# A softmax-attention front in the order queries, keys, values, with the cosine products in PSUM

## The chip, the cores and the metric

The kernel runs on one core of one Trainium2 chip. The metric is the device time of one execution in microseconds (us). Engines are named as in the profile: PE is TensorE (PEld its weight loads), DVE is VectorE, ACT is ScalarE, POOL is GpSimd, SP is SyncE.

## The reference, cut to what matters

The program is a whole stack of blocks over 512 tokens of width 1024. The change is in one mixer, which computes a multi-scale pooling and a grouped-query attention side by side from one input:

```python
z = h @ w_in                       # pooled inputs u (512), q (512), k (128), v (128)
pooled = multiscale_pool(u)        # 4 windows, one for each 128 channels
a = (pooled @ w_pool + b_pool) * pool_scale
q = apply_rope(rms_norm_2(q) * q_gain, cos, sin)    # 8 heads of 64
k = apply_rope(rms_norm_2(k) * k_gain, cos, sin)    # 2 heads of 64
p = softmax(q @ k.T * Dh ** -0.5)
y = concatenate([a, p @ v]) @ w_out
```

`apply_rope` turns even and odd channels into each other: the cosine product of the normalised input plus the sine product of its rotated copy.

## The kernel before

Activations lie with channels on the partitions and the 512 tokens along the row. Every projection is done in three passes (high times high, low times high, high times low part), all as 128x512 matmuls, except the values: those come out token-major directly, as 4 x 24 matmuls of 128 columns (kind "KV", L537).

Weights come in chunks of 256 output channels through two slots. For each chunk SP loads `raw`, ACT writes its high part `wh` (`hi_part`, L475, which waits until the chunk two before has been multiplied), and POOL writes its low part `wl` (L2164, 4.6 us for a full chunk). TensorE writes a chunk's result into one of two pairs of PSUM banks, `pairs`; four further banks are `aux`. Semaphores order everything; each engine runs its own list in the order in which the code issues it, so the functions `front_pe`, `front_act`, `front_dve` and `att_pe`, `att_act`, `att_dve` are those orders written out by hand. `linear_pe` is the general projection, with a hook `mid` between the two halves of a chunk.

Three chains (x = 0, 1, 2) normalise and rotate: before, the keys are x = 0, query tiles 0 and 1 are x = 1, query tiles 2 and 3 are x = 2. A chain is: Square on ACT, mean square on TensorE (`rope_ms_pe`, L1487), Ln and Exp on ACT (`rope_rs_act`), on DVE the normalised input qn (L1522) and the cosine product (L1526), the rotation on TensorE (`rope_rot_pe`, L1495), and on DVE the sine product (L1532) and the sum (L1537; for the keys four half-height copies, L1541). An fp32 matmul of 512 columns is two instructions in the trace, so one 1024-column mean square or rotation is "x4".

The pooling runs beside it: window sums on DVE (`pool_u_dve`, L1435 to L1444), a product on TensorE (`pool_pe`, L1450), bias and scale on DVE (L1455), high part on ACT (L1465) and low part on DVE (L1460).

The attention loop has 16 steps n, each over one pair of heads and 128 tokens: `scores` (L1576), row maximum (L1701), exponential with sum (L1639), reciprocal and multiply (L1711, L1714), eight transposes (`turn`, L1589), copy (L1648), and every second step the product with the values (`values`, L1601). Scores of step n+2 are issued before turn n. In the kernel before, chain x = 2 lies inside this loop: its mean square after the first two scores, its rotation after turn 1, its DVE parts in steps 0 and 1.

Of the kernel before, what the change touches and what calls it, by code (L numbers as in the profile page):

```python
# [20 lines left out]
P = 128  # L21
T = 512
# [28 lines left out]
for _name, _w in (("ones", P), ("ident", P), ("ntri", P), ("nones", P), ("neg_strict", P), ("keep_strict", P),  # L51
# [18 lines left out]
          ("pool_u", "F", 2), ("att_kv", "KV", 1), ("att_q", "F", 2), ("att_out", "F", 4),  # L70
# [21 lines left out]
def build(nc, xT, w2048, w1024, w1408, ada, c_d, par_d, cst_d, gla_d, rope_d, pool_d, outT):  # L92
    with ExitStack() as ctx:
# [1310 lines left out]
        AK = arena[:, 21, :]  # L1404
# [41 lines left out]
        def pool_pe(p, g):  # L1446
            p.wait_ge(u_pooled, g + 1)
            if g >= 2:
                p.wait_ge(u_out, g - 1)
            p.matmul(aux[:, g % 2, :], WPOOL[:, g * P:(g + 1) * P], UP[:, g, PAD:PAD + T], start=True, stop=True  # L1450
                     ).then_inc(u_mm, 1)

        def pool_out_dve(v, g):
            v.wait_ge(u_mm, g + 1)
            v.tensor_scalar(UP[:, g, PAD:PAD + T], aux[:, g % 2, :], pc("b_pool", g), pc("pool_scale", g),  # L1455
                            ALU.add, ALU.mult).then_inc(u_out, 1)
# [10 lines left out]

        r_sq, r_ms, r_ln, r_rs, r_qn = sem("r_sq"), sem("r_ms"), sem("r_ln"), sem("r_rs"), sem("r_qn")
# [5 lines left out]

        ROPE_SRC = [AK.rearrange("p (a t) -> p a t", a=1), AQ[:, 0:2, :], AQ[:, 2:4, :]]
        ROPE_W = [1, 2, 2]
        ROPE_MS = [aux[:, 2:3, :], aux[:, 0:2, :], aux[:, 0:2, :]]
        ROPE_ROT = [aux[:, 3:4, :], aux[:, 2:4, :], aux[:, 2:4, :]]

        def rope_ms_pe(p, x):  # L1480
            p.wait_ge(r_sq, x + 1)
            if x == 1:
                p.wait_ge(u_out, 4)
            elif x == 2:
                p.wait_ge(r_ln, 2)
            for i in range(ROPE_W[x]):
                mm = p.matmul(ROPE_MS[x][:, i, :], cm("bd64"), A_SQ[:, i, :], start=True, stop=True)  # L1487
            mm.then_inc(r_ms, 1)

        def rope_rot_pe(p, x):  # L1490
            p.wait_ge(r_qn, x + 1)
            if x:
                p.wait_ge(r_t2, x)
            for i in range(ROPE_W[x]):
                mm = p.matmul(ROPE_ROT[x][:, i, :], cm("rot"), A_QN[:, i, :], start=True, stop=True)  # L1495
            mm.then_inc(r_rot, 1)

        def rope_sq_act(a, x):
            a.wait_ge(drained, (C_KV + 1, C_Q + 1, C_Q + 2)[x])
            if x:  # L1500
                a.wait_ge(r_out, x)
            a.activation(A_SQ[:, 0:ROPE_W[x], :], ROPE_SRC[x], ACT.Square).then_inc(r_sq, 1)

        def rope_rs_act(a, x):
            a.wait_ge(r_ms, x + 1)
            rs = A_RS[:, 0:ROPE_W[x], :]
            a.activation(rs, ROPE_MS[x], ACT.Ln, scale=1.0 / 64, bias=pc("eps")).then_inc(r_ln, 1)
            a.wait_ge(r_ln, x + 1)
            a.activation(rs, rs, ACT.Exp, scale=-0.5).then_inc(r_rs, 1)

        def rope_by(x):
            return 1.0 if x else SB_D ** -0.5
# [4 lines left out]
        def rope_qn_dve(v, x):  # L1517
            v.wait_ge(r_rs, x + 1)
            if x:
                v.wait_ge(r_rot, x)  # L1520
            qn = A_QN[:, 0:ROPE_W[x], :]
            v.scalar_tensor_tensor(qn, ROPE_SRC[x], pc("q_gain" if x else "k_gain"), A_RS[:, 0:ROPE_W[x], :],  # L1522
                                   ALU.mult, ALU.mult).then_inc(r_qn, 1)
            v.wait_ge(r_qn, x + 1)
            v.wait_ge(rope_in, 16)
            v.scalar_tensor_tensor(A_T1[:, 0:ROPE_W[x], :], qn, rope_by(x), rope_table(0, x), ALU.mult, ALU.mult  # L1526
                                   ).then_inc(r_t1, 1)

        def rope_out_dve(v, x):
            v.wait_ge(r_rot, x + 1)  # L1530
            t1, t2 = A_T1[:, 0:ROPE_W[x], :], A_T2[:, 0:ROPE_W[x], :]
            v.scalar_tensor_tensor(t2, ROPE_ROT[x], rope_by(x), rope_table(1, x), ALU.mult, ALU.mult  # L1532
                                   ).then_inc(r_t2, 1)
            v.wait_ge(r_t1, x + 1)
            v.wait_ge(r_t2, x + 1)
            if x:
                v.tensor_tensor(ROPE_SRC[x], t1, t2, ALU.add).then_inc(r_out, 1)  # L1537
            else:
                for kv in range(2):
                    for r in (0, 64):  # L1540
                        ins = v.tensor_tensor(AKD[r:r + 64, kv, :], t1[kv * 64:kv * 64 + 64, 0, :],  # L1541
                                              t2[kv * 64:kv * 64 + 64, 0, :], ALU.add)
                ins.then_inc(r_out, 1)
# [5 lines left out]

        def front_pe(p):  # L1550
# [5 lines left out]
            rope_rot_pe(p, 0)  # L1556
            pool_pe(p, 2)
            pool_pe(p, 3)
            linear_pe(p, "att_q", lo=1, mid=lambda: rope_ms_pe(p, 1))
            rope_rot_pe(p, 1)  # L1560

        def att_pe(p):
            def scores(n):
                pr, tb = n // TB, n % TB
                if n == 0:
                    p.wait_ge(drained, C_Q + 1)
                    p.wait_ge(r_out, 2)
                elif n == 1:
                    p.wait_ge(drained, C_Q + 2)
                else:  # L1570
                    p.wait_ge(e_p, 2 * (n - 1))
                    if n == 2 * TB:
                        p.wait_ge(r_out, 3)
                for j in range(2):
                    r = 64 * j
                    mm = p.matmul(pairs[:, 2 * e_slot(n) + j, :], AQ[r:r + 64, pr, tb * P:(tb + 1) * P],  # L1576
                                  AKD[r:r + 64, pr // 2, :], start=True, stop=True)
                mm.then_inc(scored, 1)

            def turn(n):  # L1580
                p.wait_ge(e_pn, n + 1)
                if n:
                    p.wait_ge(e_tc, n)
                else:
                    p.wait_ge(r_ln, 3)
                for j in range(2):
# [21 lines left out]
            rope_ms_pe(p, 2)  # L1608
            for n in range(AN):
                if n + 2 < AN:  # L1610
                    scores(n + 2)
                turn(n)
                if n == 1:
                    rope_rot_pe(p, 2)
                if n % 2 == 0 and n:
                    values(n // 2 - 1)
            values(AN // 2 - 1)

        def front_act(a):
            hi_only(a, "att_kv")  # L1620
            pool_out_act(a, 0)
            pool_out_act(a, 1)
            hi_part(a, C_Q + 1, (C_Q + 1) % 2)
            rope_sq_act(a, 0)
            rope_rs_act(a, 0)
            hi_part(a, C_Q + 2, (C_Q + 2) % 2)
            rope_sq_act(a, 1)
            pool_out_act(a, 2)
            pool_out_act(a, 3)
            rope_rs_act(a, 1)  # L1630

        def att_act(a):
# [34 lines left out]
        def front_dve(v):  # L1667
            pool_u_dve(v, 0)
            pool_u_dve(v, 1)
            v.wait_ge(mm_done, C_KV + 1)  # L1670
            slot = C_KV % 2
            v.tensor_copy(AK, pairs[:, 2 * slot, :])
            v.tensor_copy(AV, pairs[:, 2 * slot + 1, :].rearrange("p (b n) -> p b n", n=P)).then_inc(drained, 1)
            pool_out_dve(v, 0)
            pool_out_dve(v, 1)
            pool_lo_dve(v, 0)
            pool_lo_dve(v, 1)
            rope_qn_dve(v, 0)
            v.wait_ge(mm_done, C_Q + 1)
            slot = C_Q % 2  # L1680
            v.tensor_scalar(AQ[:, 0:2, :], pairs[:, 2 * slot:2 * slot + 2, :], 1.0, None, ALU.mult).then_inc(drained, 1)
            pool_out_dve(v, 2)
            pool_out_dve(v, 3)
            rope_out_dve(v, 0)
            pool_lo_dve(v, 2)
            pool_lo_dve(v, 3)
            rope_qn_dve(v, 1)
            v.wait_ge(mm_done, C_Q + 2)
            slot = (C_Q + 1) % 2
            v.tensor_scalar(AQ[:, 2:4, :], pairs[:, 2 * slot:2 * slot + 2, :], 1.0, None, ALU.mult).then_inc(drained, 1)  # L1690
            rope_out_dve(v, 1)

        def att_dve(v):
# [13 lines left out]
            for n in range(AN):  # L1707
# [737 lines left out]
```

## Time and profile before

| | |
|---|---|
| median of 3 runs | 1947.4 us (1946.45 to 1948.06) |
| profiled execution | 1948.57 us, span 1946.8 us |
| PE busy | 1906.2 us (98%) |
| DVE busy | 913.0 us (47%) |
| ACT busy | 744.1 us (38%) |
| POOL busy | 770.5 us (40%) |
| granted TensorE clock, mean | 0.995 |

The span is what the trace covers; the execution's own time is 1.8 us longer. Matmuls are pipelined and their ends are modelled, so that PE's share says that it has always something to do, not that it is at its peak. The chain of waits says more: it is the path that ended last, with the engine on it at each moment.

### The profile page before, as it was taken

To read this page: it belongs to the slowest core of one execution; us is meant where nothing else is said; L and a number is where in the kernel's file an instruction comes from. 1 tells how busy PE (TensorE), PEld (TensorE's weight loads), DVE (VectorE), ACT (ScalarE), POOL (GpSimd) and SP (SyncE) were. 2 spreads that over 40 slices of the span, in tenths; PEclk is the share of its full clock that TensorE was granted. 3 is DMA by queue.
4 is the path that set the end of the run, shared out by engine and by line. 5 is a ranking of instruction groups with operands and counts; after the bars stand their busy time and mean duration, and the time that the engine had idled before them with its cause. 6 is when DMAs were issued, how large, how long until landed. Compare 5 with 4: busy or idle time off the path is not lost.

```text
span 1946.8 us, 24500 instructions
## 1 busy us (share of the span) xinstructions
PE 1906.2 (98%) x9346; PEld 1552.1 (80%) x9346; DVE 913.0 (47%) x1227; ACT 744.1 (38%) x931; POOL 770.5 (40%) x227
## 2 busy tenths in 40 slices
PE   7999999999999999979999999999999999999999
PEld 5877778878888888745888888888998778888887
DVE  5344533676614654866676415637855371111111
ACT  5444434443322335336432222234358452222221
POOL 3232314434444435200434343444486434344433
PEclk9999999999999999989999999999999999999999
DMA  5121212445435534200445345422221222223222
GB/s 200 65 75 55 78 53 66 172 151 198 149 117 195 194 119 149 85 1 9 154 184 209 110 148 212 166 96 95 96 95 63 89 105 87 88 96 109 93 78 99
DMA packets 46365, 223.90 MB, mean 115 GB/s; under 512 B 4928, under 2 KB 9280, under 8 KB 31696
## 3 DMA queue, kind: packets, MB, share of 16 engines
q1 hardware_dynamic: 33184, 174.85, 26.1%
q10 hardware_dynamic: 13104, 47.98, 6.5%
q8 instruction: 53, 0.87, 0.2%
q14 instruction: 24, 0.20, 0.0%
HBM read 220.68 MB, written 2.13 MB: 114 GB/s over the span
## 4 chain that ended last, share of the span: by engine, by line
PE 83%; DVE 5%; issue 5%; POOL 4%; ACT 2%; DMA 1%; SPq 0%; ACTq 0%; DVEq 0%; POOLq 0%
PE pairs L518 40%; PE pairs L546 18%; PE pairs L1088 4%; PE pairs L570 4%; PE pairs L537 3%; PE pairs L862 3%; PE pairs L855 2%; POOL arena L1923 2%; POOL wl L2164 2%; PE pairs L496 1%; PE aux L1601 1%; DMA raw<-in_w 1%; PE aux L920 1%; DVE aux L454 1%; DVE xl L461 1%
## 5 line engine op out<-in xcount | busy, mean ns | idle before, releaser
L2164 POOL TENSOR_TENSOR wl<-raw,wh 128x2048 fp32r<-128x2048 f32 (+2 forms) x169 | 695.5, 4115 | 1121.8 <-ACT wh L475 1121.8
L518 PE MATMUL pairs<-xh,wh 128*128 128x512 f32 x1176 | 460.3, 391 | 3.8 <-DVE aux L748 1.5
L518 PE MATMUL pairs<-xh,wl 128*128 128x512 f32 x1176 | 457.7, 389 | 0.0
L518 PE MATMUL pairs<-xl,wh 128*128 128x512 f32 x1176 | 457.7, 389 | 0.0
L475 ACT ACTIVATE wh<-raw 128x2048 fp32r<-128x2048 f32 x171 | 326.7, 1911 | 318.6 <-PE pairs L546 209.1
L518 PEld LDWEIGHTS pairs<-xh,wh 128*128 128x128 f32 x1176 | 220.9, 188 | 52.0 <-issue 3.4
L518 PEld LDWEIGHTS pairs<-xh,wl 128*128 128x128 f32 x1176 | 220.9, 188 | 47.2 <-issue 1.2
L518 PEld LDWEIGHTS pairs<-xl,wh 128*128 128x128 f32 x1176 | 220.9, 188 | 45.9
L546 PE MATMUL pairs<-zl,wh 128*128 128x512 f32 x518 | 201.6, 389 | 0.0
L546 PE MATMUL pairs<-zh,wl 128*128 128x512 f32 x518 | 201.5, 389 | 0.0
L546 PE MATMUL pairs<-zh,wh 128*128 128x512 f32 x518 | 201.5, 389 | 0.0
L787 DVE SCALAR_TENSOR_TENSOR arena<-arena,cond_row 128x1024 f32<-128x1024 f32 x96 | 188.2, 1992 | 0.0
L748 DVE TENSOR_TENSOR aux<-arena,pairs 128x512 f32<-128x512 f32 x66 | 45.9, 696 | 226.9 <-ACT arena L711 211.8
L711 ACT ACTIVATE arena<-pairs 128x512 f32<-128x512 f32 x42 | 25.1, 598 | 323.0 <-PE pairs L518 304.2
L633 DVE SCALAR_TENSOR_TENSOR h<-pairs,mod,h 128x512 f32 (+1 forms) x48 | 36.0, 751 | 226.0 <-PE pairs L546 179.5
L546 PEld LDWEIGHTS pairs<-zh,wh 128*128 128x128 f32 x518 | 97.2, 188 | 20.4
L546 PEld LDWEIGHTS pairs<-zh,wl 128*128 128x128 f32 x518 | 97.2, 188 | 20.2
L546 PEld LDWEIGHTS pairs<-zl,wh 128*128 128x128 f32 x518 | 97.2, 188 | 20.1
L751 DVE TENSOR_TENSOR zl<-aux,zh 128x512 f32 (+1 forms) x66 | 45.7, 692 | 92.3 <-ACT zh L716 92.3
L229 ACT ACTIVATE arena<-h 128x512 f32<-128x512 f32 (+1 forms) x48 | 30.1, 626 | 90.2 <-DVE h L633 59.8
L632 DVE TENSOR_TENSOR h<-pairs,h 128x512 f32 (+1 forms) x24 | 16.6, 692 | 96.7 <-PE pairs L546 81.1
L254 DVE TENSOR_TENSOR arena<-arena 128x512 f32<-128x512 f32 x48 | 54.3, 1132 | 3.4 <-ACT arena L229 3.4
(322 smaller groups left out, 2944.0 us busy)
## 6 DMA issues: line engine op xcount, KB each, us to landing
raw<-in_w SPq DMA_DIRECT2D x113, 1024.0 KB, 4.9
arena<-in_ada ACTq DMA_DIRECT2D x88, 512.0 KB, 5.4
raw<-in_w SPq DMA_DIRECT2D x48, 704.0 KB, 4.1
raw<-in_w SPq DMA_DIRECT2D x14, 512.0 KB, 3.6
arena<-in_ada SPq DMA_DIRECT2D x8, 512.0 KB, 4.9
arena<-mx_rows SPq DMA_DIRECT2D x16, 256.0 KB, 3.5
h<-in_xT SPq DMA_DIRECT2D x4, 512.0 KB, 9.0
outT<-h SPq DMA_DIRECT2D x8, 256.0 KB, 5.5
```

The costliest lines, as they stand in the source:

```text
L254: v.tensor_tensor(SQ_ACC, SQ_ACC, SQ[slot], ALU.add).then_inc(sq_acc, 1)
L475: a.activation(wh[:, slot, :], raw[:, slot, :], ACT.Copy).then_inc(hi_done, 1)
L518: mm = p.matmul(pairs[:, 2 * slot + m, :], w[:, slot, at:at + P], src[part][:, k, :], start=(k == 0 and w is wh and part == 0), stop=(k == ...
L537: mm = p.matmul(dst, src[part][:, k, tb * P:(tb + 1) * P], w[:, slot, at:at + n], start=(k == 0 and w is wh and part == 0), stop=(k == KT ...
L546: mm = p.matmul(pairs[:, 2 * slot + m, :], w[:, slot, k * P:(k + 1) * P], src[part][:, k, :], start=(k == ks[0] and w is wh and part == 0) ...
L570: mm = p.matmul(pairs[:, 2 * slot + m, :], w[:, slot, at:at + P], src[part][:, k, :], start=(k == ks[0] and w is wh and part == 0), stop=( ...
L748: v.tensor_tensor(HID[:, slot, :], ACTV[:, slot, :], pairs[:, 2 * slot + 1, :], ALU.mult).then_inc(hid_done, 1)
L751: v.tensor_tensor(zl[:, bass.ds(l, 1), :], HID[:, slot:slot + 1, :], zh[:, bass.ds(l, 1), :].bitcast(F), ALU.subtract).then_inc(drained, 1)
L787: v.scalar_tensor_tensor(ada_raw[:, at, :], ada_raw[:, at, :], 1.0, cond_row[:, :], ALU.mult, ALU.mult, accum_out=mod_raw[:, bass.ds(A, 1) ...
L862: mm = p.matmul(out, w[:, slot, at:at + P], x[:, k, :], start=(k == 0 and w is wh and x is xh), stop=(k == KT - 1 and x is xl))
L1088: mm = p.matmul(pairs[:, 2 * slot + m, :], w[:, slot, at:at + P], x[:, k, :], start=(k == 0 and w is wh and x is xh), stop=(k == KT - 1 an ...
L2164: g.tensor_tensor(wl[:, slot, 0:w], raw[:, slot, 0:w], wh[:, slot, 0:w].bitcast(F), ALU.subtract).then_inc(lo_done, 1)
```

## The change

- The chunks come in the order queries, keys and values. The chains are renumbered: query tiles 0 and 1 are x = 0, tiles 2 and 3 are x = 1, the keys x = 2. All three chains are now in the front; the loop keeps only pooling low parts and the second keys' head, on DVE in step 0.
- Queries and keys are no longer copied from `pairs` to SBUF: Square and qn read the PSUM banks, and the cosine products of the query chains are written into PSUM.
- The values are projected as the keys are, channel-major in 24 matmuls of 512 columns; ACT copies them to SBUF, TensorE turns them in four transposes, and ACT copies the result to `AV`. The first scores wait for the first of these copies (they write the same bank), the first turn for the last.
- TensorE's projections are cut in quarters (`q_pe`, `kv_pe` with `k0`, `k1`) with the chains' matmuls between them. Ln of chain 0 also waits for the fourth window's pooling, whose work space it reuses.

```diff
-          ("pool_u", "F", 2), ("att_kv", "KV", 1), ("att_q", "F", 2), ("att_out", "F", 4),
+          ("pool_u", "F", 2), ("att_q", "F", 2), ("att_kv", "KV", 1), ("att_out", "F", 4),
...
+        ROPE_SRC = [Q_BANKS[0], Q_BANKS[1], K_BANK]
...
+        ROPE_T1 = [ROPE_MS[0], Q_BANKS[1], arena[:, 26:27, :]]
...
         def rope_rs_act(a, x):
             a.wait_ge(r_ms, x + 1)
+            if x == 0:
+                a.wait_ge(u_pooled, 4)
...
+        def kv_pe(p, m, k0=0, k1=KT):
+
+            slot = C_KV % 2
+            if m == 0 and k0 == 0:
+                p.wait_ge(lo_done, C_KV + 1)
+                p.wait_ge(r_qn, 1)
+            for k in range(k0, k1):
+                for w, x in ((wh, xh), (wl, xh), (wh, xl)):
+                    at = k * 256 + m * P
+                    mm = p.matmul(V_BANK if m else K_BANK[:, 0, :], w[:, slot, at:at + P], x[:, k, :],
+                                  start=(k == 0 and w is wh and x is xh), stop=(k == KT - 1 and x is xl))
+            if k1 == KT:
+                mm.then_inc(mm_done if m else kv_half, 1)
+
+        def v_turn_pe(p):
+            p.wait_ge(drained, C_KV + 1)
+            p.wait_ge(r_ln, 3)
+            for tb in range(TB):
+                mm = p.transpose(V_TURN[:, tb * P:(tb + 1) * P], A_VT[:, tb * P:(tb + 1) * P], cm("ident"))
+            mm.then_inc(v_turned, 1)
 
         def front_pe(p):
             linear_pe(p, "pool_u", norm="n_final")
-            linear_pe(p, "att_kv")
+            q_pe(p, 0, 0)
+            q_pe(p, 0, 1)
             pool_pe(p, 0)
             pool_pe(p, 1)
-            linear_pe(p, "att_q", hi=1, mid=lambda: rope_ms_pe(p, 0))
+            q_pe(p, 1, 0, 0, 4)
+            rope_ms_pe(p, 0)
+            q_pe(p, 1, 0, 4, 8)
+            q_pe(p, 1, 1, 0, 4)
             rope_rot_pe(p, 0)
+            q_pe(p, 1, 1, 4, 8)
+            kv_pe(p, 0, 0, 4)
+            p.wait_ge(r_out, 1)
             pool_pe(p, 2)
             pool_pe(p, 3)
-            linear_pe(p, "att_q", lo=1, mid=lambda: rope_ms_pe(p, 1))
+            rope_ms_pe(p, 1)
+            kv_pe(p, 0, 4, 8)
+            kv_pe(p, 1, 0, 4)
+            rope_ms_pe(p, 2)
             rope_rot_pe(p, 1)
+            kv_pe(p, 1, 4, 8)
+            rope_rot_pe(p, 2)
+            v_turn_pe(p)
...
                 if n == 0:
-                    p.wait_ge(drained, C_Q + 1)
                     p.wait_ge(r_out, 2)
+                    p.wait_ge(drained, C_KV + 1)
                 elif n == 1:
-                    p.wait_ge(drained, C_Q + 2)
+                    p.wait_ge(r_out, 3)
...
+            a.wait_ge(mm_done, C_KV + 1)
+            a.activation(A_VT, V_BANK, ACT.Copy).then_inc(drained, C_KV + 1 - C_Q)
+            a.wait_ge(v_turned, 1)
+            a.activation(AV, V_TURN.rearrange("p (b n) -> p b n", n=P), ACT.Copy).then_inc(v_copied, 1)
```

ACT's list from the last `hi_part` of the normalisation on, before and after (L475 is `hi_part`, L1465 a pooling high part; old L1502, L1507 and L1509 are Square, Ln and Exp, and so are new L1517, L1524 and L1526):

```order
 L475 ACTIVATE wh<-raw 128x2048
+L1517 ACTIVATE arena<-pairs 128x1024
+L475 ACTIVATE wh<-raw 128x2048
+L1524 ACTIVATE arena<-aux,par 128x1024
+L1526 ACTIVATE arena<-arena 128x1024
 L1465 ACTIVATE zh<-arena 128x512 x2
-L475 ACTIVATE wh<-raw 128x2048
-L1502 ACTIVATE arena<-arena 128x512
-L1507 ACTIVATE arena<-aux,par 128x512
-L1509 ACTIVATE arena<-arena 128x512
```

The Square of the first query chunk and the high part of the keys' chunk now stand ahead of the pooling high parts, and Ln and Exp of chain 0 too.

DVE's list at the start of the attention loop in the kernel before, from the sum of chain 1 on:

```order
L1537 TENSOR_TENSOR arena<-arena 128x1024
L1701 TENSOR_REDUCE small<-pairs 128x2 x2
L1711 RECIPROCAL small<-small 128x2
L1714 TENSOR_SCALAR arena<-arena,small 128x512 x2
L1522 SCALAR_TENSOR_TENSOR arena<-arena,par 128x1024
L1526 SCALAR_TENSOR_TENSOR arena<-arena 128x1024
L1701 TENSOR_REDUCE small<-pairs 128x2
L1711 RECIPROCAL small<-small 128x2
L1714 TENSOR_SCALAR arena<-arena,small 128x512 x2
L1532 SCALAR_TENSOR_TENSOR arena<-aux,arena 128x1024
L1537 TENSOR_TENSOR arena<-arena 128x1024
```

and the same place after the change (L1767, L1777 and L1780 are row maximum, reciprocal and multiply, L1460 the pooling low parts, L1562 the second keys' head):

```order
L1555 TENSOR_TENSOR arena<-pairs,arena 128x1024
L1767 TENSOR_REDUCE small<-pairs 128x2 x2
L1777 RECIPROCAL small<-small 128x2
L1780 TENSOR_SCALAR arena<-arena,small 128x512 x2
L1460 TENSOR_TENSOR zl<-arena,zh 128x512 x2
L1562 TENSOR_TENSOR arena<-arena 64x512 x2
L1767 TENSOR_REDUCE small<-pairs 128x2
L1777 RECIPROCAL small<-small 128x2
L1780 TENSOR_SCALAR arena<-arena,small 128x512 x2
```

The four products and sums of the third query chain, of 1024 columns each, are gone from steps 0 and 1; four operations of 512 columns stand in step 0.

## Rows read from the trace of the kernel before

**Rows 1.** Chain of waits, 765 to 945: start, length (us), engine, tile, line.

```profile
796.58 5.44 PE pairs L518 x24
802.02 10.67 PE pairs L537 x96
812.69 1.77 PE aux L1450 x4
814.45 5.49 PE pairs L518 x24
...
845.94 1.73 PE aux L1495 x4
...
886.04 1.22 DVE small L1701
...
887.37 0.89 DVE arena L1714 x2
...
889.40 1.88 PE aux L1601 x16
891.28 1.08 PE pairs L1576 x4
...
892.39 1.22 DVE small L1701
...
920.75 11.13 PE pairs L570 x48
```

**Rows 2.** PE's timeline: start, length, operation [idle before, who ended it].

```profile
836.82 3.22 PE L1487 MATMUL aux<-arena,cst 128*128 128x512 f32 x4 [2.49 <-ACT arena L1502]
...
850.40 3.15 PE L1576 MATMUL pairs<-arena 64*128 64x512 f32 x8 [2.74 <-DVE arena L1537]
...
857.25 1.06 PE L1589 MATMUL aux<-cst,arena 128*128 128x128 f32 x8 [0.24 <-ACT arena L1507]
...
873.08 1.97 PE L1589 MATMUL aux<-cst,arena 128*128 128x128 f32 x8 [3.71 <-DVE arena L1714]
874.98 3.61 PE L1601 MATMUL aux<-arena 128*64 128x256 f32 x16
```

**Rows 3.** DVE's timeline, 785 to 880, the same columns.

```profile
799.00 4.96 DVE L1444 TENSOR_TENSOR arena<-arena 128x512 f32<-128x512 f32 x1
...
808.81 2.92 DVE L1435 TENSOR_TENSOR arena<-arena 128x527 f32<-128x527 f32 x4
...
830.41 5.21 DVE L1541 TENSOR_TENSOR arena<-arena 64x512 f32<-64x512 f32 x4
837.32 1.29 DVE L1460 TENSOR_TENSOR zl<-arena,zh 128x512 fp32r<-128x512 f32 x2 [1.70 <-ACT zh L1465]
...
843.64 1.23 DVE L1526 SCALAR_TENSOR_TENSOR arena<-arena 128x1024 f32<-128x1024 f32 x1
...
847.70 1.23 DVE L1532 SCALAR_TENSOR_TENSOR arena<-aux,arena 128x1024 f32<-128x1024 f32 x1 [0.49 <-PE aux L1495]
```

**Rows 4.** POOL's timeline, 785 to 880: two passes for low parts.

```profile
798.67 4.74 POOL L2164 TENSOR_TENSOR wl<-raw,wh 128x2048 fp32r<-128x2048 f32 x1 [5.53 <-ACT wh L475]
...
828.37 4.59 POOL L2164 TENSOR_TENSOR wl<-raw,wh 128x2048 fp32r<-128x2048 f32 x1 [5.41 <-ACT wh L475]
```

**Rows 5.** ACT's timeline, 785 to 880.

```profile
796.67 1.92 ACT L475 ACTIVATE wh<-raw 128x2048 fp32r<-128x2048 f32 x1 [3.10 <-PE pairs L496]
...
840.08 1.11 ACT L1507 ACTIVATE arena<-aux,par 128x1024 f32<-128x1024 f32 x1 [2.27 <-PE aux L1487]
841.23 1.06 ACT L1509 ACTIVATE arena<-arena 128x1024 f32<-128x1024 f32 x1
...
853.14 0.69 ACT L1639 ACTIVATE arena<-pairs,small 128x512 f32<-128x512 f32 x1 [1.74 <-DVE small L1701]
```

**Rows 6.** Windows: stretch, length, each engine's busy time, granted clock, DMA share, GB/s.

```profile
873.00:875.00 2.00, 1.92 (x10) 1.60 (x10) 1.97 (x5) 0.51 (x2) 0.00 (x0) 0.50 0.04 8
884.00:900.00 16.00, 15.55 (x104) 8.53 (x102) 14.39 (x26) 12.45 (x28) 0.00 (x0) 1.00 0.01 2
```

More of the change, by code:

```diff
@@ L1449, in pool_pe @@
                 p.wait_ge(u_out, g - 1)
[L1450 removed]
+            p.matmul(aux[:, 2 + g % 2, :], WPOOL[:, g * P:(g + 1) * P], UP[:, g, PAD:PAD + T], start=True, stop=True
                      ).then_inc(u_mm, 1)
@@ L1473, in build @@
         AN = ATT_H * TB // 2
[L1475 to L1478, printed above, removed]
+        kv_half = sem("kv_half")
+        Q_BANKS = [pairs[:, 2 * ((C_Q + x) % 2):2 * ((C_Q + x) % 2) + 2, :] for x in range(2)]
+        K_BANK, V_BANK = pairs[:, 2 * (C_KV % 2):2 * (C_KV % 2) + 1, :], pairs[:, 2 * (C_KV % 2) + 1, :]
+        ROPE_SRC = [Q_BANKS[0], Q_BANKS[1], K_BANK]
+        ROPE_W = [2, 2, 1]
+        ROPE_MS = [aux[:, 0:2, :], aux[:, 0:2, :], aux[:, 0:1, :]]
+        ROPE_ROT = [aux[:, 2:4, :], aux[:, 2:4, :], aux[:, 1:2, :]]
+        V_TURN = aux[:, 0, :]
+        ROPE_QN = [A_QN, A_QN, arena[:, 15:16, :]]
+        ROPE_RS = [A_RS, A_RS, arena[:, 16:17, :]]
+        ROPE_SQ = [A_SQ, A_SQ, arena[:, 28:29, :]]
+        ROPE_T1 = [ROPE_MS[0], Q_BANKS[1], arena[:, 26:27, :]]
+        ROPE_T2 = [A_RS, A_RS, arena[:, 27:28, :]]
         def rope_ms_pe(p, x):
@@ L1533, in rope_out_dve, with rope_q_dve @@
                                    ).then_inc(r_t2, 1)
+        def rope_q_dve(v, x):
             v.wait_ge(r_t1, x + 1)
             v.wait_ge(r_t2, x + 1)
[L1536 to L1543, printed above, removed]
+            v.tensor_tensor(AQ[:, 2 * x:2 * x + 2, :], ROPE_T1[x], ROPE_T2[x], ALU.add).then_inc(r_out, 1)
@@ L1546, in e_slot, with rope_k_dve, q_pe @@
+        def rope_k_dve(v, kv):
+            v.wait_ge(r_t1, 3)
+            v.wait_ge(r_t2, 3)
+            half = slice(kv * 64, kv * 64 + 64)
+            for r in (0, 64):
+                ins = v.tensor_tensor(AKD[r:r + 64, kv, :], ROPE_T1[2][half, 0, :], ROPE_T2[2][half, 0, :], ALU.add)
+            ins.then_inc(r_out, 1)
         def e_slot(n):
             return (n + C_Q) % 2
+        def q_pe(p, l, m, k0=0, k1=KT):
+            c = C_Q + l
+            slot = c % 2
+            if m == 0 and k0 == 0:
+                p.wait_ge(lo_done, c + 1)
+                p.wait_ge(drained, c - 1)
+            for k in range(k0, k1):
+                for w, x in ((wh, xh), (wl, xh), (wh, xl)):
+                    at = k * 256 + m * P
+                    mm = p.matmul(pairs[:, 2 * slot + m, :], w[:, slot, at:at + P], x[:, k, :],
+                                  start=(k == 0 and w is wh and x is xh), stop=(k == KT - 1 and x is xl))
+            if m == 1 and k1 == KT:
+                mm.then_inc(mm_done, 1)
```

111 lines of the change are left out of this document (57 added, 54 removed).

## The prediction

> **What bounds the kernel now.** Read the page first: TensorE (PE) is busy nearly all of the span, so a microsecond can only be won where it waits or where its own work shrinks. The change touches one stretch, from the end of the last projection of the pooled inputs (796.58) to the first matmul of att_out (920.75) [rows 1]. Read there the chain of waits. Up to 829 it is TensorE end to end. The keys-and-values chunk costs it 5.44 us for the keys and 10.67 us for the values, which use 96 matmuls of 128 columns [rows 1]. After that the gaps begin; PE's timeline names them. At 836.82 it had waited 2.49 us for ACT's Square of queries 0 and 1, at 850.40 it had waited 2.74 us for DVE's last addition, and at 873.08 3.71 us for the probabilities [rows 2]. The last is in the softmax loop: the third query chain (qn, cosine, rotation, sine, sum of query tiles 2 and 3) sits inside it. Once it is gone, two steps of the loop take 892.39 - 886.04 = 6.35 us, a circle of values, scores, row maximum, multiply and turn, without a longer wait [rows 1]. From turn 0 (857.25) to turn 2 (873.08) they take 15.83 [rows 2].
>
> What to see besides: after such gaps the granted clock is 0.50 of full, the 1.2 GHz level, as in 873 to 875, and it is 1.00 in 884 to 900 [rows 6]. Four matmul instructions that take 1.73 us at full clock [rows 1] then take up to 3.22 [rows 2].
>
> **The front, walked.** I lay durations of rows end to end in the new order of each engine, with about 0.04 us from one engine to the next as the chain shows. The same walk over the old order puts the first scores at 850.42 and the end at 920.85; the trace has 850.40 and 920.75, so the method is good to a few tenths.
>
> PE: from 796.58 two query halves of 5.49 [rows 1] end at 807.5; the pooling products (1.77) [rows 1] and two quarters plus the mean squares plus one quarter (2.74, 1.73, 2.74, 2.74; a quarter is half of 5.49) bring it to 819.2. It then wants the first rotation's input.
>
> ACT: Square of query chunk 0 reads PSUM, 1.08 by L1507's 1.11 and L1509's 1.06 [rows 5], so 807.5 to 808.65; then the high part of the keys' chunk, 1.92 [rows 5], to 810.5.
>
> GpSimd: the low part starts there and takes 4.6 [rows 4], to 815.1. Before, only the pass at 798.67 met the window sums, and no other came before they were done. Now a second one does: DVE is in the fourth window's sums, four L1435 adds from 808.81 [rows 3]. An add with both inputs in SBUF that begins during a GpSimd pass does not end until the pass has: L1444 at 799.00 took 4.96 us and ended at 803.96, the pass at 803.41; the first L1541 at 830.41 had to wait too (four of them took 5.21) for the pass that ended at 832.96 [rows 3, 4]. So the fourth add ends at 815.7 and the last two operations (0.73 each) at 817.2, where the old order had 813.2. The changed Ln of chain 0 waits for all four windows.
> The Trainium skill has this as a rule (SBUF — State Buffer, section SBUF: two separate sides): a DVE op with two SBUF inputs and a GpSimd op take turns on one port pair, each for its whole length. It speaks against this change, and the trace agrees with it by the 4.96 us. Taken to the letter the third add, already running, would also push GpSimd to 811.0 and the sum 0.5 later.
>
> Then Ln and Exp (1.11, 1.06) reach 819.4, qn 1.23, rotation from 820.7 to 822.45. TensorE has waited 1.5 us. From there its own work is 20.6 us: five quarters are 13.7, the pooling products 1.7, mean squares and rotation of queries 2 x 1.73, of keys 2 x 0.86. I checked what it waits for: queries 0 and 1 done 825.6 against 827.9 when needed; second qn 834.9 against 837.7; keys' qn 839.9 against 842.2. It ends at 843.07. DVE's sine and two key copies (0.7 each, by the two L1460 in 1.29 [rows 3]) give the first scores at 845.25. ACT's copy of the values, four transposes (half of 1.06 [rows 2]) and the copy back end at 844.25, covered by that same DVE work; without that cover they would be 1.2 us after the rotation anyway. **Term A: 850.40 - 845.25 = 5.15 us.** It is almost the 5.2 that the values save on TensorE (10.67 - 5.49); the old waits of 2.49 and 2.74 go, and 1.5, 2.2 and the key additions take their place.
>
> DVE's reads from PSUM instead of a copy in SBUF I cost at nothing extra: 1.23 us for 1024 columns with a PSUM input (L1532), as for L1526 with none [rows 3]. 
>
> **The loop.** Scores 0 to turn 0: before 857.25 - 850.40 = 6.85 [rows 2]. Now scores 1.06, row maximum 1.22, exponentials about 1.4 (two of 0.69 with a read of the sum) [rows 5], reciprocal and multiply 1.1 [rows 1]: 845.25 to 850.14, 4.9. **Term B: 1.95.**
> Turn 0 to turn 2: DVE now does there two low parts (1.29) [rows 3] and two key additions (1.4), 850.0 to 852.5, which hold up row maximum 2; nothing of the query chain is left. The walk gives turn 1 at 854.7 and turn 2 at 856.88, 6.74 us, near the steady 6.35. **Term C: 15.83 - 6.74 = 9.09.**
> Turn 2 and the first values ran at the low clock, 1.97 and 3.61 [rows 2], against 1.06 for turn 0 [rows 2] and 1.88 in the steady part [rows 1]. **Term D: 2.6.** From there to 920.75 the order is unchanged, and what follows shifts with it: the weights of att_out are ready by 833, seventy microseconds ahead.
> A + B + C + D = 18.8.
>
> **Term E, the low clock in the new order.** The trace of before cannot show it. The new gaps are shorter: 1.5 before the first rotation, 1.6 and 1.5 around scores 0 and 1, about 1.2 in step 1, against the 2.49, 2.74 and 3.71 ahead of slow rows [rows 2]. Bounds: nothing; or twice what one stretch cost (2.6), 5.2. TensorE is thinly used between 844 and 855 all the same, so I take 1.5, what the first old stretch cost (3.22 - 1.73), towards the low end because the gaps are nearer to those at full clock. Sum 18.8 - 1.5 = **17.3 us**. On the profiled execution, 1948.57, that is 1931.3; it lies 1.2 above the median of 1947.4, so the forecast is 1930.1, rounded to **1930.0**.
>
> **Rivals.**
> 1. The clock stays low through the thin part and the first rotation falls in it too: E is 5.2 and 1.7 more. 18.8 - 6.9 = 11.9, time 1935.5. For it: only 2.1 us of work between 844 and 848. Against: the shorter gaps.
> 2. The GpSimd pass misses the sums (ACT takes the keys' chunk later, or DVE goes first). Then the 1.5 before the rotation goes: 17.3 + 1.5, time 1928.6.
> 3. The front gains but the loop does not speed up, since low parts and key additions hold step 0 as the query chain did: A alone, 5.15, time 1942.2. Against: 2.7 us of DVE work replace five operations of 1.23 to 1.29 with a rotation and two ACT passes between them.
> 4. Slower. Without the query chain's matmuls TensorE may never get back to full clock in the loop. A pair of steps has two scores, two turns and the values, 2 x 1.08 + 2 x 1.06 + 1.88 = 6.2 us of PE work [rows 1, 2]; at half clock that is 12.3, 6.0 more than the 6.35 of now. Seven pairs are 42, less the 17.3: time about 1972. It decides beyond 2.9 pairs. Against: at this very spacing the granted clock was 1.00 for 16 us [rows 6].
> 5. Nothing comes of it: the first scores wait for the values' copy (they share a bank) and ACT is late. It would have to be 17 us late, with 1 us of slack; 1947.
>
> **How the numbers follow.** Forecast 0.66 (own range 1928.5 to 1933), rival 1 0.15, rival 2 0.07, rival 3 0.07, rival 4 0.03, rival 5 0.02. Within 0.2% (3.9 us) is about what a measurement cannot tell from no change. Faster is then 0.95, same 0.02, slower 0.03. The range holds the forecast and rivals 1 and 2. Below, E = 0 with rival 2 gives 18.8 + 1.5 = 20.3, 1927.1; above, rival 1 gives 1935.5: 1926.5 to 1936.0.
>
> **What the profile would show.** Attention's first scores at 845 to 847; a fourth or fifth L1435 add of 4 to 5 us at 811 and chain 0's Ln at 817; TensorE idle 1.5 us before the first rotation; turn 2 about 11.6 us after the first scores; two steps in 6.35 us afterwards; att_out at 902 to 905. Wrong would be: turn 2 more than 16 us after the scores (rival 3), or granted clock under 1 beyond turn 4 (rivals 1, 4).

## The result

The changed kernel takes 1931.28 us (median of 4 runs, 1930.27 to 1932.73) against 1947.73 of the kernel before, measured beside it (4 runs, 1946.45 to 1948.16): a ratio of 0.992, 95% interval 0.9907 to 0.9932. Its profiled execution took 1930.47 us, 18.1 less than the 1948.57 of before.

The page of the changed kernel:

```profile
span 1928.6 us, 24365 instructions
## 1 busy us (share of the span) xinstructions
PE 1897.9 (98%) x9278; PEld 1545.8 (80%) x9278; DVE 909.2 (47%) x1223; ACT 745.6 (39%) x933; POOL 770.0 (40%) x227
```

The chain of waits of the changed kernel, 765 to 945, answering to [rows 1]:

```profile
811.14 4.98 DVE arena L1444
816.20 1.13 ACT arena L1524
...
819.78 1.98 PE aux L1507 x4
821.76 2.77 PE pairs L1580 x12
824.53 2.72 PE pairs L1594 x12
...
861.45 1.23 DVE small L1767
...
867.79 1.22 DVE small L1767
...
902.51 11.13 PE pairs L570 x48
```

The first matmul of att_out starts at 902.51 instead of 920.75. That is 18.24 us, and the span is 18.2 shorter, so nothing behind this stretch took part. Ahead of it this profile lost a little: TensorE starts its first matmul of the stretch 0.58 us later than in the profile before:

```profile
796.41 0.39 PE L518 MATMUL pairs<-xh,wh 128*128 128x512 f32 x1
```

```profile
796.99 0.39 PE L1580 MATMUL pairs<-xh,wh 128*128 128x512 f32 x1
```

The first line is of the kernel before, the second of the changed one. Two steps of the loop take 867.79 - 861.45 = 6.34 us.

PE's timeline of the changed kernel, answering to [rows 2] (start, length, operation, idle before):

```profile
844.61 3.09 PE L1645 MATMUL pairs<-arena 64*128 64x512 f32 x8 [1.72 <-DVE arena L1562]
...
850.55 1.97 PE L1659 MATMUL aux<-cst,arena 128*128 128x128 f32 x8
...
855.10 1.09 PE L1659 MATMUL aux<-cst,arena 128*128 128x128 f32 x8 [1.28 <-DVE arena L1780]
...
857.40 1.06 PE L1659 MATMUL aux<-cst,arena 128*128 128x128 f32 x8
858.39 1.95 PE L1671 MATMUL aux<-arena 128*64 128x256 f32 x16
```

The gain by the marks of the prediction: first scores 850.40 - 844.61 = 5.79; scores to turn 0 take 5.94 instead of 6.85; turn 0 to turn 2 take 857.40 - 850.55 = 6.85 instead of 15.83, 8.98 less; turn 2 to att_out 45.11 instead of 47.67, 2.56 less. About half of the gain is that the third query chain no longer stands bare in the loop.

Windows of the changed kernel (columns as in [rows 6]):

```profile
784.60:798.00 13.40, 13.40 (x53) 10.87 (x53) 12.84 (x21) 5.58 (x7) 4.62 (x1) 0.87 0.24 78
...
846.00:853.00 7.00, 6.16 (x18) 2.74 (x20) 6.06 (x10) 3.34 (x9) 0.00 (x0) 0.51 0.00 0
853.00:902.00 49.00, 44.03 (x298) 24.87 (x296) 38.06 (x70) 36.71 (x75) 0.00 (x0) 1.00 0.00 1
```

The low clock still shows, at the start of the loop (0.51), but the rest of the loop has 1.00. The first row is ahead of the change, and it matters below.

### The profile page after: what moved, and what is told of

Its sections match the earlier page's. It is cut to its first block, busy times and chain, and to the rows that moved or that the text cites. A ratio compares the mean times of both kernels' runs of the same rounds, so it can differ in the third digit from the quotient of the medians.

```text
span 1928.6 us, 24365 instructions
## 1 busy us (share of the span) xinstructions
PE 1897.9 (98%) x9278; PEld 1545.8 (80%) x9278; DVE 909.2 (47%) x1223; ACT 745.6 (39%) x933; POOL 770.0 (40%) x227
## 4 chain that ended last, share of the span: by engine, by line
PE 82%; DVE 6%; issue 5%; POOL 4%; ACT 2%; DMA 1%; SPq 0%; ACTq 0%; DVEq 0%; POOLq 0%
PE pairs L518 40%; PE pairs L546 19%; PE pairs L1088 4%; PE pairs L570 4%; PE pairs L862 3%; PE pairs L537 2%; PE pairs L855 2%; POOL arena L1989 2%; POOL wl L2230 2%; PE pairs L496 1%; PE aux L1671 1%; DVE aux L454 1%; PE aux L920 1%; DMA raw<-in_w 1%; DVE xl L461 1%
## 5 line engine op out<-in xcount | busy, mean ns | idle before, releaser
L475 ACT ACTIVATE wh<-raw 128x2048 fp32r<-128x2048 f32 x171 | 326.7, 1911 | 313.9 <-PE pairs L546 209.0
L518 PE MATMUL pairs<-xh,wh 128*128 128x512 f32 x1136 | 442.5, 389 | 3.8 <-DVE aux L748 1.5
L518 PE MATMUL pairs<-xl,wh 128*128 128x512 f32 x1136 | 442.0, 389 | 0.0
L518 PE MATMUL pairs<-xh,wl 128*128 128x512 f32 x1136 | 442.0, 389 | 0.0
L518 PEld LDWEIGHTS pairs<-xh,wh 128*128 128x128 f32 x1136 | 213.2, 188 | 49.6 <-issue 2.1
L518 PEld LDWEIGHTS pairs<-xl,wh 128*128 128x128 f32 x1136 | 213.2, 188 | 44.2
L518 PEld LDWEIGHTS pairs<-xh,wl 128*128 128x128 f32 x1136 | 213.2, 188 | 44.1
```

The lines of the kernel that those rows point to most:

```text
L475: a.activation(wh[:, slot, :], raw[:, slot, :], ACT.Copy).then_inc(hi_done, 1)
L518: mm = p.matmul(pairs[:, 2 * slot + m, :], w[:, slot, at:at + P], src[part][:, k, :], start=(k == 0 and w is wh and part == 0), stop=(k == ...
```

## The same kernel took two courses through the front

The expected stall is there, but on another operation. DVE's and POOL's timelines of the changed kernel, answering to [rows 3, 4]:

```profile
798.78 0.69 DVE L1444 TENSOR_TENSOR arena<-arena 128x512 f32<-128x512 f32 x1
...
800.63 5.34 DVE L1435 TENSOR_TENSOR arena<-arena 128x527 f32<-128x527 f32 x3
...
811.14 4.97 DVE L1444 TENSOR_TENSOR arena<-arena 128x512 f32<-128x512 f32 x1
```

```profile
799.25 4.69 POOL L2230 TENSOR_TENSOR wl<-raw,wh 128x2048 fp32r<-128x2048 f32 x1 [6.32 <-ACT wh L475]
810.98 4.58 POOL L2230 TENSOR_TENSOR wl<-raw,wh 128x2048 fp32r<-128x2048 f32 x1 [7.04 <-ACT wh L475]
```

The addition that lost 4.3 us before, at 799.00, now starts 0.47 us ahead of the pass and takes 0.69. The pass holds the third window's additions instead: three take 5.34, where in the profile before they took 2.19. The second pass catches the window's last operation and holds it to 816.11, 0.55 after its own end.

**a_again** is the changed kernel once more, with a second profile; its times also stand for the changed kernel beside the experiments.

> The changed kernel as it is, once more. Theory: 1931.3 within 1.5 us again, and the front's profile may differ by a few tenths in where DVE's window sums meet the GpSimd pass of the keys' chunk: the fourth window is ready between 812 and 817.5. If that meeting sets the time, executions fall into two groups about 1.5 us apart; if it does not, they spread evenly within about 1 us. Rival: none for the median.

Measured: 1932.55 us (5 runs, 1929.34 to 1933.73) against 1946.96 of before (10 runs), ratio 0.9925 (0.9912 to 0.9939). The five runs spread over 4.4 us without two groups in them, so neither of the two expected pictures came out. The profiled execution took 1933.73, 3.3 us longer than the other. DVE, POOL and PE in it, and its window ahead of 798:

```profile
798.82 4.98 DVE L1444 TENSOR_TENSOR arena<-arena 128x512 f32<-128x512 f32 x1
...
808.64 7.17 DVE L1435 TENSOR_TENSOR arena<-arena 128x527 f32<-128x527 f32 x4
```

```profile
798.49 4.76 POOL L2230 TENSOR_TENSOR wl<-raw,wh 128x2048 fp32r<-128x2048 f32 x1 [5.53 <-ACT wh L475]
810.22 5.04 POOL L2230 TENSOR_TENSOR wl<-raw,wh 128x2048 fp32r<-128x2048 f32 x1 [6.96 <-ACT wh L475]
```

```profile
820.94 3.34 PE L1507 MATMUL aux<-arena,cst 128*128 128x512 f32 x4 [2.00 <-DVE arena L1538]
...
829.91 1.88 PE L1450 MATMUL aux<-arena 128*128 128x512 f32 x4
...
847.42 3.32 PE L1645 MATMUL pairs<-arena 64*128 64x512 f32 x8 [1.73 <-DVE arena L1562]
```

```profile
784.60:798.00 13.40, 13.02 (x56) 10.27 (x57) 12.84 (x21) 6.38 (x7) 4.61 (x1) 1.00 0.23 78
```

Read the two side by side. Here the granted clock before 798 was 1.00, and all of TensorE's and ACT's work at 797 came 0.76 earlier (`hi_part` at 796.49 against 797.25). So the pass started first, at 798.49, and L1444 at 798.82 waited it out. The other profile lost 3.15 us to the same pass in the third window; here the loss was 4.3, and DVE came to its fourth window 1.2 us later (808.64 against 807.46). There it met the second pass with the additions themselves: four took 7.17 instead of 2.92. Ln started at 817.36, 1.2 later. TensorE was ready at 818.94, idled 2.00, and ran the rotation at the low clock, 3.34 against 1.98 (granted clock 0.57 from 821 to 825). The matmuls behind it were slow too: from the rotation's start to the pooling product of L1450 it took 8.97 us, against 7.31 in the other profile (819.78 to 827.09). The first scores came at 847.42, 2.8 later than in the other profile: 1.2 by the sums and 1.7 by the low clock. att_out came at 905.55, 3.0 later. So a TensorE that was 0.76 us early went with 3 us lost. That the one led to the other is read from the two profiles; no run sets the start of the first pass by itself.

## Experiments

All times are medians. e_v_tokens, e_hi_late and e_k1_late were taken beside a_again and the kernel before at 1946.96 us; e_filler, e_v_only and e_chain_first beside before at 1946.7 (21 runs); e_copy_q, e_hi_gated, e_best and e_best2 beside before at 1946.85 (9 runs) on another chip. The changed kernel itself was not run on that chip.

### e_v_tokens: the values as before, in the new order

```diff
-            kv_pe(p, 1, 0, 4)
+            v_pe(p, (0, 1))
...
-            kv_pe(p, 1, 4, 8)
+            v_pe(p, (2, 3))
-            v_turn_pe(p)
```

`v_pe` writes two token tiles each, in 48 matmuls of 128 columns.

> The changed kernel with the values projected token-major as before (96 matmuls of 128 columns) and copied straight to AV, without the transposes. Theory (from the first rotation on the front is TensorE's own work, so the values' projection is priced in full): 10.67 - 5.49 = 5.2 us slower than the changed kernel, about 1936.5, first scores at about 849.8. Rival (the front is set by the chains and the values' saving is hidden): 1931 to 1932, first scores at 845.

Measured: 1939.15 us (1936.08 to 1939.79), ratio 0.9959 (0.9946 to 0.9972): 6.6 over a_again. PE:

```profile
820.83 1.98 PE L1507 MATMUL aux<-arena,cst 128*128 128x512 f32 x4 [2.03 <-DVE arena L1538]
...
828.12 1.88 PE L1450 MATMUL aux<-arena 128*128 128x512 f32 x4
...
850.89 3.63 PE L1656 MATMUL pairs<-arena 64*128 64x512 f32 x8 [2.27 <-DVE arena L1562]
```

The rotation waited 2.03 us as in a_again, but ran at full clock here, so the pooling product of L1450 comes 1.79 earlier. From it to the first scores the front takes 850.89 - 828.12 = 22.77 us, against 847.42 - 829.91 = 17.51: 5.26 more, which is what the values' new form is worth to the front, the 5.2 of the old rows. The time is 2.6 above the 1936.5 expected, since the loop is slower too, which the expectation did not have: first scores to turn 2 took 14.95 instead of 13.03, where turn 1 ran at the low clock as well (1.97 against 1.09), and turn 2 to att_out 46.05 instead of 45.10.

### e_v_only: only the values, on the kernel before

```diff
-                if kind in ("T", "KV"):
+                if kind == "KV":
+                    for k in range(KT):
+                        for w, part in passes:
+                            at = k * 256 + P
+                            mm = p.matmul(pairs[:, 2 * slot + 1, :], w[:, slot, at:at + P], src[part][:, k, :],
...
-            linear_pe(p, "att_q", hi=1, mid=lambda: rope_ms_pe(p, 0))
+            linear_pe(p, "att_q", hi=1, mid=lambda: (rope_ms_pe(p, 0), v_turn_pe(p)))
```

DVE copies the values and ACT the turned ones.

> The kernel before with one part of the change alone: the values projected channel-major in 24 matmuls of 512 columns, copied by DVE, turned by TensorE in chain 0 and copied by ACT. Theory (the saving needs the new order): TensorE is 5.2 us ahead after the keys and values, but the mean square of chain 0 waits for ACT's Square, which waits for DVE's copies behind the window sums until 814.4; 4 to 5 of the 5.2 are lost there. 1946 to 1947.5. Rival (the saving stands by itself): 1942.5.

Measured: 1946.8 us (10 runs, 1943.71 to 1950.45), ratio 1.0003 (0.9993 to 1.0014). PE:

```profile
817.53 1.13 PE L1496 MATMUL aux<-arena,cst 128*128 128x512 f32 x2 [2.26 <-ACT arena L1511]
...
835.12 2.81 PE L1496 MATMUL aux<-arena,cst 128*128 128x512 f32 x4 [2.49 <-ACT arena L1511]
```

The same 5.2 us of TensorE work are gone, and nothing measurable is won by the medians. In the profile TensorE now waits 2.26 us for the keys' Square, where it had waited for nothing, the four transposes take 0.6, and the stretch began 0.6 later; the 2.49 at the next mean square stood there before. First scores come at 848.70, only 1.7 earlier. The saving needs something to put into those waits. How much of that is the order and how much the copies by DVE, which this run keeps ahead of Square, it does not tell apart.

### e_chain_first: only the third chain ahead of the loop, on the kernel before

```diff
             rope_rot_pe(p, 1)
+            rope_ms_pe(p, 2)
+            rope_rot_pe(p, 2)
```

with its ACT and DVE parts moved alike.

> The kernel before with the third query chain taken out of the loop and put ahead of the first scores, where no projection covers it. Theory (the chain costs the same wherever it is exposed; the changed kernel gains because it lies under projections): first scores about 12 us later, at 862 to 863, the loop then 12 us shorter as in the changed kernel: 1946 to 1949. Rival (the loop's form was the fault, and being out of it is enough): 1936 to 1938.

Measured: 1947.41 us (10 runs, 1945.97 to 1949.6), ratio 1.0004 (0.9995 to 1.0014). PE:

```profile
851.93 3.78 PE L1487 MATMUL aux<-arena,cst 128*128 128x512 f32 x4 [3.79 <-ACT arena L1502]
...
859.32 3.78 PE L1495 MATMUL aux<-arena,cst 128*128 128x512 f32 x4 [3.61 <-DVE arena L1522]
```

The loop is as quick as after the change (turn 0 at 870.37 to turn 2 at 876.69: 6.3), but the chain stands bare ahead of it: two waits of 3.8 and 3.6 us and two stages of 3.78 at the low clock. It costs the same outside the loop as in it. What the change wins is not the place but the cover: the key and value projections lie over the query chains' waits.

### e_copy_q: the query chunks copied to SBUF first

```diff
-        ROPE_SRC = [Q_BANKS[0], Q_BANKS[1], K_BANK]
+        ROPE_SRC = [AQ[:, 0:2, :], AQ[:, 2:4, :], K_BANK]
...
+            q_copy_dve(v, 0)
             pool_out_dve(v, 0)
```

Square, and with it the chain, waits for this copy; the second query chunk likewise.

> The changed kernel with the query chunks copied to SBUF by DVE first, as before the change, and Square and qn reading the copy. Theory (reading PSUM directly frees the chain from DVE's window sums): the Square of chain 0 waits for the copy behind the sums, at 813 instead of 808; TensorE waits 2 us for it and up to 1 us for the rotation's input: 1933.5 to 1935. Rival (the direct read gives nothing, the slack covers the copy): 1931 to 1932.5.

Measured: 1934.9 us (4 runs, 1934.15 to 1935.48), ratio 0.9939 (0.9924 to 0.9954). DVE and PE:

```profile
812.42 1.22 DVE L1530 TENSOR_SCALAR arena<-pairs 128x1024 f32<-128x1024 f32 x1
```

```profile
814.78 3.78 PE L1497 MATMUL aux<-arena,cst 128*128 128x512 f32 x4 [3.56 <-ACT arena L1517]
```

The copy itself is 1.22 us, but it stands behind the fourth window on DVE, so Square and with it TensorE wait (3.56 us and then the low clock). Reading PSUM directly takes DVE out of the path from projection to Square. By the medians it is worth 2.4 us against a_again, which ran on another chip. The nearer comparison is e_hi_gated below, on the same chip: here the keys' pass started at 816.60, behind the window sums, as it does there, so both lack the stall, and the copies cost 1934.9 - 1930.55 = 4.4 us.

### e_hi_late and e_hi_gated: the keys' pass away from the window sums

e_hi_late puts `hi_part` of the keys' chunk behind Ln and Exp of chain 0; e_hi_gated leaves it in place, behind a wait for the fourth window:

```diff
             rope_sq_act(a, 0)
+            a.wait_ge(u_pooled, 4)
             hi_part(a, C_KV, C_KV % 2)
             rope_rs_act(a, 0)
```

> The changed kernel with ACT's high part of the keys' chunk behind Ln and Exp of chain 0, so that its GpSimd pass starts after the window sums. Theory: no window operation takes 4 to 5 us, the fourth window is ready at about 812, Ln of chain 0 waits for its mean square (814) and TensorE has its rotation input by 818, before it wants it. Worth what TensorE waited there, 0.1 in this profile and up to 1.5 by the forecast's walk: 1929.8 to 1931.2. The pass then ends at about 823 and delays the pooling low parts, not the keys' projection (824.5). Rival (the pass is late for the keys' projection): slower by 1 or more.

> The changed kernel with one wait added on ACT: the high part of the keys' chunk waits for the fourth window's pooling, so that its GpSimd pass runs in 814 to 818.5, while DVE works from PSUM. Theory (the meeting of pass and window sums makes the slower of the two kinds of execution): no DVE operation of the front over 4 us except the one at the first pass (799 to 804), first scores at 844.3 to 845, all executions within 2 us of each other, median 1930.0 to 1931.0. Rival (the two kinds come from elsewhere, as the clock): executions spread from 1929.3 to 1933.7 as for the changed kernel.

Measured: e_hi_late 1931.16 us (1929.62 to 1931.51), ratio 0.9922 (0.9908 to 0.9935); e_hi_gated 1930.55 (1928.65 to 1931.2), ratio 0.9915 (0.9902 to 0.9929). POOL, DVE and PE in e_hi_late:

```profile
818.71 5.12 POOL L2230 TENSOR_TENSOR wl<-raw,wh 128x2048 fp32r<-128x2048 f32 x1 [14.44 <-ACT wh L475]
```

```profile
819.33 5.66 DVE L1460 TENSOR_TENSOR zl<-arena,zh 128x512 fp32r<-128x512 f32 x2
```

```profile
827.89 1.98 PE L1450 MATMUL aux<-arena 128*128 128x512 f32 x4 [0.66 <-DVE arena L1555]
```

The fourth window was done at 812.2 and the rotation found its input, but the pass then fell on the pooling low parts, two of which took 5.66 instead of 1.29; what was left of the delay reached TensorE as 0.66 us. In e_hi_gated the pass ran from 814.19 to 818.81 and met only an operation that took 1.75 instead of 1.23; TensorE waited for nothing from 819.86 to its 1.72 us before the first scores, and the granted clock from 846 to 856 was 1.00. Against a_again the two medians are 1.4 and 2.0 lower, against the changed kernel's first median 0.1 and 0.7. The intervals overlap, and e_hi_gated ran on another chip. So the times put the stall at anything from nothing to 2 us, although the two profiles differ by 3. The expectation had also asked for executions within 2 us of each other if the meeting makes two kinds of them; they spread over 2.55, so this test did not settle it.

### e_k1_late: the second keys' head in step 4

```diff
+                if n == 4:
                     rope_k_dve(v, 1)
```

> The changed kernel with the second keys' head added up in step 4 of the loop instead of step 0. Theory (DVE's work in step 0 sets the second row maximum): step 0 is 1.4 us shorter, turn 2 up to 1.4 earlier after the first scores; step 4 has 0.7 us of idle DVE to take the 1.4, so 0.5 to 1.0 us faster in all, 1930.5. Rival (something else, as the low clock, sets step 1): no change, 1931.3, or slower by 0.7.

Measured: 1929.66 us (1928.96 to 1930.63), ratio 0.9917 (0.9903 to 0.993). DVE:

```profile
862.14 1.39 DVE L1562 TENSOR_TENSOR arena<-arena 64x512 f32<-64x512 f32 x2
```

Turn 0 to turn 2 fell from 6.85 to 5.54 us, 1.3, which is these two additions; turn 2 to att_out rose from 45.11 to 45.90, 0.8, since in the steady loop they delay a row maximum as well. About 0.5 us remains by the profile. The median is 1.6 below the changed kernel's first and 2.9 below a_again, more than that; the intervals overlap, and what makes the rest is not shown.

### e_filler: extra matmuls into an unused bank at the start of the loop

```diff
+            p.wait_ge(r_t2, 3)
+            filler(p, 6)
...
+                if n < 2:
+                    filler(p, 4)
```

Each is one matmul of 512 columns whose result nothing reads.

> The changed kernel with matmuls that serve nothing (0.23 us each at full clock) in an unused PSUM bank: six before the first scores, four before each of scores 2 and 3, to keep TensorE at work. Theory (the low clock of the loop's start costs 1.5 to 2.5 us): granted clock 1.00 from 842 to 860, the first two scores together 2.1 us instead of 3.1, 1929 to 1930. Rival (the low clock's cost is hidden behind DVE and ACT): 1931.3 or slower by the fillers that stand in the way, up to 1 us.

Measured: 1931.89 us (1929.52 to 1934.6), ratio 0.9925 (0.9911 to 0.9939): a_again's. Windows of a_again and of e_filler:

```profile
846.00:856.00 10.00, 7.84 (x24) 3.29 (x24) 8.78 (x13) 3.85 (x10) 0.00 (x0) 0.66 0.00 0
```

```profile
846.00:856.00 10.00, 8.97 (x38) 4.21 (x37) 9.48 (x13) 3.99 (x10) 0.00 (x0) 1.00 0.00 0
```

The granted clock rose from 0.66 to 1.00 and first scores to turn 2 fell from 13.03 to 12.35 us. So the low clock there was worth 0.7 on the path, below the 1.5 to 2.5 expected: turn 1 waited 1.91 us for DVE anyway. The rotation stood ahead of the extra matmuls and ran at the low clock here too (0.59 from 821 to 825). In e_hi_gated, at full clock without filler, the stretch takes 12.35 too (844.55 to 856.90).

### e_best and e_best2: the edits that paid, together

e_best is e_hi_gated with the pooling low parts 2 and 3 moved into the front behind the second cosine product, and the second keys' head in step 3. e_best2 also moves the keys' rotation forward:

```diff
-            kv_pe(p, 1, 4, 8)
+            kv_pe(p, 1, 4, 6)
             rope_rot_pe(p, 2)
+            kv_pe(p, 1, 6, 8)
             v_turn_pe(p)
```

> The same, with DVE's step 0 of the loop emptied: the low parts of pooling groups 2 and 3 between the second cosine product and the keys' qn in the front, where DVE waited 2.9 us, and the second keys' head in step 3, where it waited 1.8. Theory: row maximum 2 starts 2.7 us earlier, or as soon as scores 2 are there; turn 0 to turn 2 takes 5.5 instead of 6.85 and nothing is given back: 1928.5 to 1929.5. Rival (scores 2 at the low clock come no earlier, and the rest is given back as in the run with the head in step 4): 1930.0 to 1930.5.

> The same as the one before, and the keys' rotation cut in before the last quarter of the values' projection. Theory (TensorE's 1.7 us before the first scores are DVE's sine and additions behind the rotation): they run under the last matmuls of the values, the first scores wait for the values' copy and turn only, 1.0 us earlier: 1927.5 to 1928.5. Rival (keys' qn comes too late for the earlier place, TensorE waits there instead): no gain over the one before.

Measured: e_best 1927.82 us (4 runs, 1926.44 to 1928.09), ratio 0.9903 (0.9888 to 0.9918); e_best2 1925.31 (4 runs, 1925.29 to 1925.33), ratio 0.989 (0.9874 to 0.9905). PE and a window of e_best2:

```profile
838.72 1.02 PE L1507 MATMUL aux<-arena,cst 128*128 128x512 f32 x2
841.87 0.66 PE L1603 MATMUL aux<-cst,arena 128*128 128x128 f32 x4 [0.75 <-ACT arena L1703]
842.46 1.99 PE L1646 MATMUL pairs<-arena 64*128 64x512 f32 x8
...
847.51 1.09 PE L1660 MATMUL aux<-cst,arena 128*128 128x128 f32 x8
...
852.17 1.09 PE L1660 MATMUL aux<-cst,arena 128*128 128x128 f32 x8
```

```profile
846.00:856.00 10.00, 9.31 (x56) 4.83 (x56) 8.99 (x17) 8.70 (x21) 0.00 (x0) 1.00 0.00 0
```

With the rotation earlier, sine and key copies lie under the last quarter of the values, and the first scores start without a wait, 2.15 us before the changed kernel's. Turn 0 to turn 2 is 4.66 us, against 6.85. The value transposes now wait 0.75 us for their copy, the cover that the prediction named. The mean granted clock is 1.000 over the whole span, and the four runs lie within 0.04 us. Its interval lies just below that of the changed kernel. Both times lie under their expectations, by 0.7 and 2.2 us. In the profiles the rotation's move brought the first scores 1.08 us forward (843.54 to 842.46), as expected; the medians differ by 2.5. Moving the low parts was not tried by itself.

## Why the prediction was right

- **Forecast and rivals.** The time lies 1.3 us above the forecast of 1930.0, within its own range, and so does the 1932.55 of a_again; the profiled execution of a_again, 1933.73, lies 0.7 above the range. That the number came so near is in part luck: att_out moved forward by 18.2 us in one profile and by 15.2 in the other, and the forecast of 17.3 lies between two courses of which it had walked one. Rivals 3, 4 and 5 did not occur: the loop ran at 6.34 per pair, its clock was 1.00 from 853 on, and the values' copy had slack. (Rival 3 counts five operations of the third chain on DVE; there are four.) Rival 1 occurred in one part: in a_again the rotation fell in the low clock and cost 1.7, as priced. Rival 2 was built as e_hi_gated: 1930.55, and not the 1928.6 of its price.
- **Term A, 5.15, measured 5.79 in one profile and 2.98 in the other.** The walk with the stall of the fourth addition is what a_again shows: sums done at 817.26 (walk 817.2), Ln at 817.36 (817), TensorE idle 2.00 (1.5), rotation at 820.94 (820.7). Its first scores still came 2.2 after the walk's 845.25, 1.7 of it by the low clock in and behind the rotation, which the prediction had priced outside term A. The other profile took a course that the walk did not have: the first pass started 0.47 us behind L1444 instead of ahead of it, and TensorE waited for nothing before the rotation, so that the 1.5 in term A did not occur. Its 5.79 agrees with 5.15 by luck as much as by the walk; counted from the stretch's own start, 0.58 later, it is 6.4. From the rotation on the walk held: 24.83 us to the first scores in it, against 24.55. e_v_tokens puts the part of the values' form at 5.26, and e_v_only shows that it is worth nothing in the old order as built there.
- **The stall itself.** The prediction's row on it held in both profiles: 4.97 and 7.17 for operations of 0.69 and 2.92. The Trainium skill (SBUF — State Buffer, section SBUF: two separate sides) says that the two engines take turns on the shared port, each holding it for a whole operation; the trace agrees, also for the engine that comes second when it is GpSimd: its pass took 5.04 us instead of 4.6 when DVE's addition had started before it. The prediction had set that case aside at 0.5 us; it was 0.44, and the sums still ended on the walk's time since the pass began 0.3 us earlier than walked. An operation with one of its two inputs in PSUM ran in its usual 1.28 us inside a pass (L1538 at 816.98 in e_best2, pass 814.93 to 819.55).
- **Terms B and E.** B less E was forecast at 0.45 and measured at 0.91 in the profile. B is 1.8 at full clock (first scores to turn 0 is 5.06 in e_hi_gated, forecast 4.9). E was forecast at 1.5; it was 0.4 in the first profile (12.79 against 12.35 from scores to turn 2) and 0.68 + 1.66 = 2.3 in a_again, where the rotation fell in it. The bounds held, and 1.5 lies between the two courses; the reason given for it, the length of the gaps, does not tell them apart, since the same gap of 2.0 us before the rotation was followed by the low clock in a_again and e_filler and by full clock in e_v_tokens.
- **Term C, 9.09, measured 8.98**, and **term D, 2.6, measured 2.56**. At full clock turn 0 to turn 2 took 7.29 in e_hi_gated, 0.55 more than walked. 0.2 of that is in the walk's own sum: 1.29 and 1.4 are 2.7, and it laid 2.5 (850.0 to 852.5). The rest was not traced. The low clock makes turn 0 late and leaves turn 1, which waits for DVE, where it was, so C looks better at the low clock (6.85) than at full (7.29). Scores to turn 2 was walked at 11.63 and took 12.35 at full clock; the 0.7 was covered by an E that was 1.1 too large for this profile. e_k1_late and e_best confirm what holds it: with the two additions gone 5.54, with the low parts gone as well 4.67.
- **Costed at nothing.** The reads from PSUM cost nothing extra (1.28 for qn with a PSUM input), and e_copy_q shows that the way they replace is dearer, 4.4 us against e_hi_gated. The transposes and both copies of the values did not delay the scores.

What stays open: why the granted clock before 798 was 0.87 to 0.89 in six of the profiles (the changed kernel's first, e_hi_late, e_hi_gated, e_k1_late, e_v_only and e_chain_first) and 1.00 in the other seven, the kernel's before among them, with the same code there (in all six L1444 started ahead of the pass at 799, in all seven behind it); and how often an execution without a trace takes either course. The changed kernel's runs spread over 1929.3 to 1933.7, about what the two profiles differ by, but that this is their cause is argued and not shown.

## What to carry to other kernels

A chain of small operations over several engines costs the same wherever nothing lies beside it (1947.4 with the chain before the loop, 1946.7 with it inside); it becomes cheap when TensorE's next projection is cut in pieces and laid over its waits. Work saved on the busiest engine counts only where that engine isn't waiting next: the same 5.2 us were worth nothing in the old order and 5.3 (front of the profiles) to 6.6 (medians) in the new one. Look where a GpSimd pass meets a DVE operation on two SBUF inputs on the path, and give the pass a place behind it with a wait, rather than leave a start within 0.5 us of it to chance; here that was worth between nothing and 2 us by the times.

## What the runs showed of the hardware that was not expected

- Two profiles of one kernel differed by 3.3 us; in the slower a GpSimd pass started 0.33 us before a DVE addition, in the quicker 0.47 after it. The execution with the lower clock ahead of that place was the quicker one. In all 13 profiles the granted clock before 798 and the order of the two went together: 0.87 to 0.89 with the addition first, 1.00 with the pass first.
- The four executions of e_best2, each with a mean granted clock of 1.000, lay within 0.04 us; those of the other kernels spread over 1.3 to 6.7. The profile of e_best2 has neither such a meeting on the path nor the low clock in the loop; that this is why is not shown.
- TensorE rows at the low clock (3.09 for the first scores, 1.97 for a turn) lengthened the loop's start by 0.4 to 0.7 us in all, since DVE was the later of the two.
